# Output projection of a two-layer block split along its input, one half issued inside the recurrence

## The reference, cut to what matters

```python
fox_out = fox_attention(...)                       # features 0..511 of the mixer
rec, _  = hgrn2_chunkwise(gq, gf, gi, lb)          # the recurrence: 4 heads of 128, features 512..1023
rec = rmsnorm(rec, hgrn_norm_g) * silu(gg)
h = h + concatenate([fox_out, rec], -1) @ w_out    # 1024 x 1024, 512 tokens: the output projection
mem_n = rmsnorm(mem, norm_mem_g)                   # 256 memory tokens
h = h + memory_cross_attention(rmsnorm(h, norm_x_g), mem_n, w_xq, w_xkv, w_xo)
```

## Time and profile before

| | |
|---|---|
| median of 3 runs | 2276.75 us (2276.06 to 2281.61) |
| the profiled execution, its own time | 2282.82 us |
| its span in the profile | 2281.1 us |
| granted clock over the span | 0.963 |
| PE busy | 2130.7 us, 93% |
| DVE, ACT, POOL busy | 1157.3, 713.1 and 866.5 us |
| recurrence, first product to last head output | 267.7 to 344.9 us |
| norm of its heads | to 361.9 us |
| projection by `w_out` | to 410.2 us |
| units of `w_xkv` | to 465.5 us |

### The profile page before, as it was taken

The page is one execution under the profiler, slowest core; times in us unless marked ns, Lnnn a source line. Parts: engine busy times, 40 slices in busy tenths (PEclk is TensorE's granted clock), DMA queues, the critical chain, the costliest instruction groups (busy, mean ns, idle before and its releaser), DMA issues.

```text
span 2281.1 us, 26706 instructions
## 1 busy us (share of the span) xinstructions
PE 2130.7 (93%) x10150; PEld 1710.0 (75%) x10150; DVE 1157.3 (51%) x1880; ACT 713.1 (31%) x976; POOL 866.5 (38%) x456
## 2 busy tenths in 40 slices
PE   6999868999899999989988999999899988999998
PEld 5877667976678878865356888888788767888887
DVE  4145684524687886556536676632665664111112
ACT  4243533423322222333433212222344323213221
POOL 2322332641344444435022444444344433444442
PEclk8999888999999999988998999999999999999999
DMA  4322003430455553221014555522223112233222
GB/s 131 102 70 70 10 1 111 130 111 22 152 177 184 180 176 104 93 88 56 1 56 148 170 193 177 178 93 93 76 91 109 61 37 74 93 103 99 92 88 79
DMA packets 223966, 232.56 MB, mean 102 GB/s; under 512 B 4195, under 2 KB 218932, under 8 KB 223740
## 3 DMA queue, kind: packets, MB, share of 16 engines
q1 hardware_dynamic: 223868, 231.22, 31.1%
HBM read 228.96 MB, written 2.24 MB: 101 GB/s over the span
## 4 chain that ended last, share of the span: by engine, by line
PE 81%; DVE 10%; ACT 3%; issue 3%; POOL 1%; DMA 1%; SPq 0%; DVEq 0%; ACTq 0%; PEldq 0%
PE ps L1836 23%; PE ps L1838 22%; PE ps L1837 22%; POOL wL L582 1%; PE ps L2326 1%; PE ps L1946 1%; PE ps L1964 1%; ACT wH L707 1%; PE ps L2340 1%; DVE adacc L1494 1%; PE ps L2047 1%; PE ps L2067 1%; DVE hnL L1165 1%; PE ps L1913 1%; DVE T L1178 1%
## 5 line engine op out<-in xcount | busy, mean ns | idle before, releaser
L582 POOL TENSOR_TENSOR wL<-raw,wH 128x1024 fp32r<-128x1024 f32 (+2 forms) x322 | 772.9, 2422 | 1268.2 <-ACT wH L707 1268.1
L1836 PE MATMUL ps<-hnH,wH 128*128 128x512 f32 x1344 | 540.0, 402 | 22.2 <-DVE hnL L1165 14.1
L1838 PE MATMUL ps<-hnH,wL 128*128 128x512 f32 x1344 | 530.6, 395 | 0.0
L1837 PE MATMUL ps<-hnL,wH 128*128 128x512 f32 x1344 | 530.2, 395 | 0.0
L707 ACT ACTIVATE wH<-raw 128x2048 fp32r<-128x2048 f32 (+2 forms) x161 | 302.5, 1879 | 554.8 <-PE ps L1838 528.3
L1836 PE MATMUL ps<-uH,wH 128*128 128x512 f32 x864 | 341.7, 395 | 9.2 <-DVE uL L1163 8.8
L1838 PE MATMUL ps<-uH,wL 128*128 128x512 f32 x864 | 338.3, 392 | 0.0
L1837 PE MATMUL ps<-uL,wH 128*128 128x512 f32 x864 | 338.3, 392 | 0.0
L1836 PEld LDWEIGHTS ps<-hnH,wH 128*128 128x128 f32 x1344 | 257.3, 191 | 81.8 <-issue 19.4
L1838 PEld LDWEIGHTS ps<-hnH,wL 128*128 128x128 f32 x1344 | 256.5, 191 | 55.6
L1837 PEld LDWEIGHTS ps<-hnL,wH 128*128 128x128 f32 x1344 | 257.0, 191 | 52.7 <-issue 1.2
(11 more groups left out here) (345 smaller groups left out, 2414.1 us busy)
## 6 DMA issues: line engine op xcount, KB each, us to landing
raw<-in_ffn_w_dram SPq DMA_DIRECT2D x60, 1024.0 KB, 5.1
adaw<-in_ada_w_dram SPq DMA_DIRECT2D x48, 1024.0 KB, 7.2
raw<-in_w_dram SPq DMA_DIRECT2D x32, 1024.0 KB, 5.4
raw<-in_w_in_dram SPq DMA_DIRECT2D x14, 1024.0 KB, 5.4
raw<-in_od_w_in_dram SPq DMA_DIRECT2D x12, 1024.0 KB, 5.3
raw<-in_w_xkv_dram SPq DMA_DIRECT2D x8, 1024.0 KB, 5.4
raw<-in_ffn_w_dram SPq DMA_DIRECT2D x8, 768.0 KB, 4.2
raw<-in_ev_w_in_dram SPq DMA_DIRECT2D x5, 1024.0 KB, 5.2
```

Of the source, the lines that this page charges most:

```text
L582: nc.gpsimd.tensor_tensor(wL[n % 2][:, k0:k1, 0:c], raw[n % 2][:, k0:k1, 0:c], wH[n % 2][:, k0:k1, 0:c].bitcast(F32), ALU.subtract).then_i ...
L1836: nc.tensor.matmul(out_ap, wh, xh, start=first, stop=False)
L1837: nc.tensor.matmul(out_ap, wh, xl, start=False, stop=False)
L1838: return nc.tensor.matmul(out_ap, wl, xh, start=False, stop=last)
```

## The change

The four units of `w_out` become eight of half the input (4 chunks each), first the four over the forget-gate half, then the four over the recurrence's half. PE issues the first four inside the recurrence, from the generator `output_beside`: after each of the 32 products one chunk of one block, three matmuls of 128x512. Their blocks lie in banks 4 and 5, so the products of the levels go round banks 2 and 3 alone. DVE adds each of the 8 blocks to `xT` in the recurrence (`residual_beside`), and adds the 8 blocks of the second half behind it, 16 in all instead of 8. SP loads, and ACT and POOL split, one half unit per head there. The memory is loaded earlier, to another place, and squared by ACT in heads 1 and 2; its scaling by DVE moves ahead of the first residual. The second four units wait chunk by chunk (`chunks_of`) instead of for all. The memory's transposes stand behind units 0 and 1 of the second four.

```diff
@@ -62,8 +62,9 @@
     for c0 in (1024, 1280, 2056, 2312, 2568, 2824, 1544, 1800, 3080, 3336):
         add("w_in", 0, KC, c0, UC)
     stage("out")
-    for c0 in range(0, D, UC):
-        add("w_out", 0, KC, c0, UC)
+    for k0 in (0, KC // 2):
+        for c0 in range(0, D, UC):
+            add("w_out", k0, KC // 2, c0, UC)
...
+    if OUT_FILL[0] <= b < OUT_FILL[1]:
+        return 4 + b % 2
     return 4 + b % 2 if V_FILL[0] <= b < V_FILL[1] else b % 4
 
 
 def last_in_bank(b):
 
-    return b - 2 if FOX_FILL[0] <= b < FOX_FILL[1] or V_FILL[0] + 2 <= b < V_FILL[1] else b - 4
+    return b - 2 if FOX_FILL[0] <= b < OUT_FILL[1] or V_FILL[0] + 2 <= b < V_FILL[1] else b - 4
...
             sp.wait_ge(op_lo, Q0["mix"] + 4)
             sp.dma_start(lvl[:], a["levels"].rearrange("l s t -> s l t")).then_inc(lvl_in, 16)
-
-            sp.wait_ge(op_lo, Q0["mix"] + 8)
+            load(AT["out"][0] + 1)
             for mb in range(2):
                 sp.dma_start(mtok[:, mb, :], a["mem"][0, mb * P:(mb + 1) * P, :]).then_inc(mem_in, 16)
-            loads(AT["out"][0] + 1, AT["ff1"][0])
+            loads(AT["out"][0] + 2, AT["ff1"][0])
...
+                    if l == 2:
+                        low(AT["out"][0] + 1 + h)
...
-            lows(AT["out"][0] + 1, AT["ff1"][0])
+            lows(AT["out"][0] + 5, AT["ff1"][0])
...
+                    if l == 1:
+                        high(AT["out"][0] + 1 + h)
+                    if l == 5 and h in (1, 2):
+                        act.wait_ge(mem_in, 32)
+                        nc.scalar.activation(mdump[:], mtok[:, h - 1, :], ACT.Square, accum_out=mstat[:, h - 1:h]).then_inc(astep, 1)
+                        acts[0] += 1
...
+            act.wait_ge(astep, acts[0])
+            nc.scalar.activation(mstat[:, 4:6], mstat[:, 0:2], ACT.Sqrt, bias=eps, scale=1.0 / D).then_inc(m_root, 1)
...
-            n = AT["out"][0]
+            n = AT["out"][0] + 4
             high(n + 1)
-            act.wait_ge(mem_in, 32)
-            for mb in range(2):
-                chain(nc.scalar.activation(mdump[:], mtok[:, mb, :], ACT.Square, accum_out=mstat[:, mb:mb + 1]))
-            nc.scalar.activation(mstat[:, 4:6], mstat[:, 0:2], ACT.Sqrt, bias=eps, scale=1.0 / D).then_inc(m_root, 1)
+
+            def memory_high(js):
+                for j in js:
+                    high_op(Q0["mem"] + j, memH[:, j, :], mT[j % 2][:], (m_t, j + 1))
+
+            memory_high(range(0, 4))
             high(n + 2)
-            for half in range(2):
-                high(n + 3 + half)
-                for j in range(4 * half, 4 * half + 4):
-                    high_op(Q0["mem"] + j, memH[:, j, :], mT[j % 2][:], (m_t, j + 1))
-                squares("x", BLOCK0[n], range(2 * half, 2 * half + 2))
-            m = AT["xkv"][0]
+            memory_high(range(4, KC))
+            squares("x", BLOCK0[n], range(0, 2))
+            high(n + 3)
+            squares("x", BLOCK0[n], range(2, 4))
+            high(n + 4)
             squares("x", BLOCK0[n], range(4, 6))
-            high(m + 1)
+            high(n + 5)
...
-                                          ps[2 + e % 4][:].rearrange("p (c t) -> p c t", c=TB)).then_inc(h_at, 1)
+                                          ps[2 + e % 2][:].rearrange("p (c t) -> p c t", c=TB)).then_inc(h_at, 1)
...
+            def residual_beside(j):
+
+                bb = OUT_FILL[0] + j
+                dve.wait_ge(blk_done, bb + 1)
+                nc.vector.tensor_tensor(xT[:, j, :], ps[bank(bb)][:], xT[:, j, :], ALU.add).then_inc(blk_taken, 1)
...
+                    if l == 1 and h:
+                        residual_beside(2 * h - 1)
+                    if l == 5:
+                        residual_beside(2 * h)
...
+            residual_beside(KC - 1)
...
+            dve.wait_ge(m_root, 1)
+            chain(nc.vector.reciprocal(mstat[:, 2:4], mstat[:, 4:6]))
+            for mb in range(2):
+                nc.vector.tensor_scalar(mtok[:, mb, :], mtok[:, mb, :], mstat[:, 2 + mb:3 + mb], None, ALU.mult).then_inc(m_n, 1)
+            b = OUT_FILL[1]
             for j in range(KC):
                 residual(b + j, j)
-                if j == 1:
-                    dve.wait_ge(m_root, 1)
-                    chain(nc.vector.reciprocal(mstat[:, 2:4], mstat[:, 4:6]))
-                    for mb in range(2):
-                        nc.vector.tensor_scalar(mtok[:, mb, :], mtok[:, mb, :], mstat[:, 2 + mb:3 + mb], None, ALU.mult).then_inc(m_n, 1)
-                if j in (3, 5):
-                    for jj in range(2 * j - 6, 2 * j - 2):
+                if j in (1, 3):
+                    for jj in range(2 * j - 2, 2 * j + 2):
                         memory_chunk(jj)
-                if j in (3, 5):
-                    norm_add("x", j - 3)
-                    norm_add("x", j - 2)
-                if j == 6:
-                    norm_add("x", 4)
-                    norm_add("x", 5)
+                if j in (3, 5, 6):
+                    norm_add("x", {3: 0, 5: 2, 6: 4}[j])
+                    norm_add("x", {3: 1, 5: 3, 6: 5}[j])
...
+            def output_beside():
+
+                pe.wait_ge(mx_done, FOX_H * TB)
+                pe.wait_ge(op_lo, Q0["mix"] + 4)
+                for u in range(AT["out"][0], AT["out"][0] + 4):
+                    unit_ready(u)
+                    unit_whole(u)
+                    for c in range(2):
+                        b = BLOCK0[u] + c
+                        cs = slice(c * P, (c + 1) * P)
+                        bank_free(b)
+                        for k in range(KC // 2):
+                            ins = parts(ps[bank(b)][:], (wH[u % 2][:, k, cs], wL[u % 2][:, k, cs]), (uH[:, k, :], uL[:, k, :]),
+                                        k == 0, k == KC // 2 - 1)
+                            if k == KC // 2 - 1:
+                                ins.then_inc(blk_done, 1)
+                            yield
+
+            beside = output_beside()
...
-                    if e >= 4:
-                        pe.wait_ge(h_at, e - 3)
+                    if e >= 2:
+                        pe.wait_ge(h_at, e - 1)
...
+                    next(beside, None)
...
-            n = AT["out"][0]
-            feature_unit(n, uH, uL, need=all_chunks_of(Q0["mix"]))
-            for u in range(1, 4):
-                feature_unit(n + u, uH, uL)
-                if u == 3:
-                    break
-                pe.wait_ge(m_n, 2)
-                for j in range(4 * u - 4, 4 * u):
-                    if j >= 4:
-                        pe.wait_ge(op_lo, Q0["mem"] + j - 3)
-                    for mb in range(2):
-                        ins = nc.tensor.transpose(ps[4 + j % 4][:, mb * P:(mb + 1) * P], mtok[:, mb, j * P:(j + 1) * P], ident)
-                    ins.then_inc(m_tr, 1)
+                broadcast(hrs[:, 4 * h:4 * h + 4], (5, 6, 7, 4)[h]).then_inc(h_bc, 1)
+
+            n = AT["out"][0] + 4
+            for u in range(4):
+                feature_unit(n + u, uH[:, KC // 2:KC, :], uL[:, KC // 2:KC, :], need=chunks_of(Q0["mix"] + 4) if u == 0 else None)
+                if u < 2:
+                    pe.wait_ge(m_n, 2)
+                    for j in range(4 * u, 4 * u + 4):
+                        if j >= 4:
+                            pe.wait_ge(op_lo, Q0["mem"] + j - 3)
+                        for mb in range(2):
+                            ins = nc.tensor.transpose(ps[4 + j % 4][:, mb * P:(mb + 1) * P], mtok[:, mb, j * P:(j + 1) * P], ident)
+                        ins.then_inc(m_tr, 1)
```

More of the change, by code:

```diff
@@ L120 @@
 FOX_FILL = (BLOCK0[FOX_UNIT], BLOCK0[AT["out"][0]])
+OUT_FILL = (BLOCK0[AT["out"][0]], BLOCK0[AT["out"][0] + 4])
 V_FILL = (BLOCK0[AT["od_in"][0] + 10], BLOCK0[AT["od_in"][0] + 13])
@@ L301, in bass_block_pair @@
     lvl = place("lvl", [P, 8, P], F32, AR + 8192)[0]
-    ho = place("ho", [P, HG_H, S], F32, AR + 12288)[0]
+    ho = place("ho", [P, HG_H, S], F32, AR)[0]
     dd = R + [place(f"dd{i}", [P, S], F32, HN + 2048 * i)[0] for i in range(HG_RING - 2)]
@@ L314, in bass_block_pair @@
     memL = place("memL", [P, KC, M_MEM], F32R, AR + 8192)[0]
-    mtok = place("mtok", [P, 2, D], F32, AR + 49152)[0]
+    mtok = place("mtok", [P, 2, D], F32, AR + 16384)[0]
     xk = place("xk", [P, KC, M_MEM], F32, AR + 16384)[0]
@@ L318, in bass_block_pair @@
     xq = place("xq", [P, KC, S], F32, AR + 32768)[0]
-    mdump = place("mdump", [P, D], F32, HN)[0]
+    mdump = place("mdump", [P, D], F32, AR + 12288)[0]
     xdump = place("xdump", [P, D], F32, AR + 20480)[0]
@@ L1426, in _ @@
                     dve.wait_ge(op_lo, Q0["mix"] + 4 + h - 1)
-                nc.vector.tensor_tensor(T[h % 2][:], ps[(5, 6, 7, 2)[h]][:], gg[:, h, :], ALU.mult).then_inc(op_t, 1)
+                nc.vector.tensor_tensor(T[h % 2][:], ps[(5, 6, 7, 4)[h]][:], gg[:, h, :], ALU.mult).then_inc(op_t, 1)
                 low_op(Q0["mix"] + 4 + h, uL[:, 4 + h, :], T[h % 2][:], uH[:, 4 + h, :])
@@ L2103, in _ @@
```

(20 more changed lines are left out.)

## The result

| | before | after |
|---|---|---|
| median of the runs | 2277.47 us (4 runs, 2276.06 to 2281.61) | 2264.16 us (4 runs, 2261.61 to 2266.47) |
| ratio, 95% interval | | 0.9933 [0.9918, 0.9948] |
| the profiled execution, its own time | 2282.82 us | 2266.47 us |
| its span, granted clock | 2281.1 us, 0.963 | 2264.8 us, 0.969 |

The change gains 13.3 us between the medians, 0.58%; by the ratio it is 0.67%. A second comparison, of 5 runs with 9, gave 2265.94 against 2278.16, ratio 0.9940 [0.9926, 0.9954].

What follows compares the result with a forecast made beforehand. DVE was taken to bound the recurrence, PE the projection, a buffer ring `w_xkv`. Recurrence +10.0, behind -22.9, `w_xkv` +0.5 gave -12.4 us: 2270.4 profiled, median 2264, range 2254 to 2274.

Steps and rivals of the forecast that it cites:

- additions: DVE in the recurrence: eight new additions of 0.69 us, seven on DVE's path, +4.8 us.
- lows: POOL in the recurrence: four half-size lows stretch DVE instructions with both inputs in SBUF, 1.5 us a head, +6.0 us.
- border of heads: PE in the recurrence: with two banks the diagonal step stands behind one more chunk, 0.5 us each, +1.5 us.
- faster clock: Recurrence: more matmuls bring PE's clock nearer 1, giving back a third of DVE's 7.1 us of waiting, -2.3 us.
- behind: Projection behind the recurrence: PE ends at 387.3 instead of 410.2, a gain of 22.9 us.
- `w_xkv`: Ring of buffers in the `w_xkv` units: half units leave less time to load ahead, 0.5 us lost, from 0 to 2.
- The three short waits: PE behind the recurrence: waits 1 us for `mtok`, 0.9 before unit 3 and 2.9 before unit 4.
- the offset of 6.1 us: Whole kernel: profiled execution lies 6.1 us above the median, so 2270.4 profiled becomes a median of 2264.
- Lows and clock cost nothing: Recurrence: low falls into POOL's gap, clock stays at 1, growth 4 us or less; gain 19, 2258; chance 0.22.
- PE bounds the recurrence: Recurrence: PE at half clock half of the time, growth 18 us; gain 4 to 5, 2272; chance 0.14.
- The second half is ACT's and DVE's: Projection's second half: memory chunks, squares, sums and roundings share 22 us, PE ends at 392; gain 7, 2269; chance 0.09.
- ACT stands still: Recurrence: ACT's rounding waits for PE, delaying what queues behind; slower if growth exceeds 22.4 us; chance 0.05.

Runs made afterwards that it cites:

- thin additions: Changed kernel with the eight residual additions in the recurrence cut to 8 of 512 tokens: recurrence 80.7 us, span 2259.5 us.
- thin lows: Changed kernel with POOL's four lows in the recurrence cut to 8 of 256 columns of each chunk: recurrence 79.6 us, span 2264.2 us.
- both thin: Changed kernel with both the lows and the additions of the recurrence cut to 8 columns and 8 tokens: recurrence 74.7 us, span 2253.4 us.
- matmuls alone: Kernel before, products round two banks, plus three unread matmuls after each of the 32 products: 2271.36 us, ratio 0.9983.
- all half units behind: Changed kernel with all eight half units behind the recurrence, their roundings, lows and additions there too: 2280.77 us, ratio 1.0003.

## Why the prediction was right, and where its terms were off

The forecast was 2264 (2254 to 2274), and 2264.16 was measured, faster by more than 0.3%. By its terms, all in us:

| term | forecast | measured | by what |
|---|---|---|---|
| additions | +4.8 | +3.5 to +4.9 | thin additions |
| lows | +6.0 | +4.6 to +6.0 | thin lows |
| border of heads, less the faster clock | -0.8 | -2.4, not clear of the norm's spread | both thin, 85.5 against 87.9 |
| recurrence with norm | +10.0 | +8.0 (6.9 to 8.7) | three profiles against two |
| behind | -22.9 | -22.2 | 26.3 against 48.5 |
| `w_xkv` | +0.5 | -1.5 | 54.4 against 56.0 |
| sum | -12.4 | -15.7 | |

*The mechanism held.* DVE bounds the recurrence (busy 91% of it), PE's matmuls went in without a wait, and the projection lost its first half. ACT's rounding waited for PE where the prediction said. It had its start at 304.3, when PE would be done with the block; it began at 307.62. The step was right and its time 3.3 us early: the product from which I counted stood at 303.43 and not at 300.4, for the levels ahead of it already carried additions and longer instructions, and from it to the rounding it was 4.2 us where I had counted 3.9.

*Behind.* The three short waits were forecast as 1.0, 0.9 and 2.9 us and measured 0.93, 0.84 and 2.62. `mtok` took 2.45 us for the pair. `mtok` was done 2.6 us behind the last `uL` (367.31 to 369.88) where I had 3.2, and the clock was at half behind the longest wait, which I had not counted: 7 matmuls in 3.12 us (386.55 to 389.67) instead of 1.6, 1.5 us. So the stage took 26.3 us where 25.5 was forecast.

*The clock.* The third of DVE's waiting (2.3 us) that I let it give back was the term with the weakest ground. DVE's wait for products was 7.1 and 3.8 us in the two profiles of before and 6.7 to 7.2 in the three of after, so it was not given back there. What the clock may have given is seen only over recurrence and norm together, 2.4 us with the matmuls alone, and is no more than the norm's own spread. The 0.5 us per border that I charged for two banks does not show.

*Two readings of the rows.* In the earlier trace rows the subtraction of 309.08 (1.16 us) ran beside POOL's multiply of 308.96, for `kd` only began at 309.65; the multiply of 310.16 (1.48 us) is the one beside `kd`. And the `mT` of 395.33 in the earlier trace rows lies behind POOL's low, which ended at 393.82. The trace has one beside the low, at 391.50, with 0.47 us, so what I said of instructions that read PSUM stands, as it does for the addition of 310.02.

*`w_xkv`.* The ring has the same steps as in the earlier trace rows: in the chain of after, ACT 1.93 and POOL 5.23 us. The 0.5 us of lateness did not show; instead the stage was 0.7 to 2.4 us shorter than in the two profiles of before (55.1 and 56.8), just below the 55 to 57 that I had named as a sign. The spread of the two is 1.7 us.

*The step that failed.* It is the one from the profile to the median. I let the offset of 6.1 us between the profiled execution and the median stand for both kernels. Before, it was indeed 5.3 us (2282.82 against 2277.47) and 7.1 (2285.29 against 2278.16); after, only 2.3 (2266.47 against 2264.16) and 0.7 (2266.65 against 2265.94). Between profiles the change gained 17.5 us (mean spans 2282.3 and 2264.8) where I forecast 12.4. The stages above give 15.7 of it, a start of the recurrence 1.4 us earlier another 1.4, and all that follows `w_xkv` 0.4. The earlier start is no work of the change: thin lows, with the change, began as late as before (267.6), and the matmuls alone, without it, as early as after (266.1). So the sum was off by 5 us and the offset by nearly as much the other way, and the hit to 0.2 us is luck. The offset is most likely the spread of the executions: 29 of the kernel before took from 2269.87 to 2284.05 us, and its two profiled ones, 2282.82 and 2285.29, lie at and just past the slow end of that. The clock of the second was lower than in eight of the nine runs beside it (0.961 against 0.964 to 0.968); where in the program those ran faster has no trace.

*The rivals.* "Lows and clock cost nothing" is out: the lows cost 4.6 us or more. "PE bounds the recurrence" is out at a clock of 0.98. "The second half is ACT's and DVE's" is out with 26.3 us, though its mechanism is what makes the third wait. "ACT stands still" happened three times, for at most 4.5 us, but exponentials late by that much were mostly covered: with both lows and additions thin, ACT still waits 3.8 us three times and does all its roundings, and the recurrence takes 74.7 us, against 74.2 with the matmuls alone.

## What to carry to other kernels

Look for a stage where the matrix engine is the one waited for, and a stage before it where another engine is and the inputs of some of that work are ready; moving the work was worth its full matmul time here (22.2 us for 96 matmuls of 0.227), less what its helpers (additions, splits) take on the engine that bounds the stage. Price those helpers by the instructions that they stretch on that engine, not by their own engine's idle time. Put a forecast against sums over stages that trade time with each other, profile the same code more than once before a difference of 2 us is called a gain, and don't carry the offset of one profiled execution over to the other kernel.

## What the runs showed of the hardware

96 extra matmuls whose result nobody reads cost the DVE-bound recurrence nothing: with its norm it took 85.0 us against 87.4, at a granted clock of 0.97 instead of 0.82, and the whole kernel had a ratio of 0.9983 [0.9968, 0.9998] to before. The gain itself is no larger than the spread of the norm. The norm, with 51 to 57 matmuls, takes 10.7 to 10.9 us at a clock of 0.71 to 0.73, 12.0 to 12.3 at 0.63 or 0.64, 13.2 and 13.3 at 0.61 and 0.62, and 13.9 at 0.50. Where a stretch of half clock falls thus moved 3 us between two neighbouring stages of the kernel before, and 2.5 us in and out of the norm of the changed one.

A rest of PE of 2.62 us was followed by half clock in the changed kernel, and one of 2.63 us in the kernel with all half units behind. Rests of 0.84, 0.93, 0.95 and, in the latter, 2.08 us were not: behind that last one the matmuls are 0.23 us apart (365.70 to 365.93). With the longest rest gone the projection and the stage behind it ran at 1.00.

Four POOL subtractions of two instructions each, 11.9 us, lengthened DVE's instructions in the same stretch by 3.9 us in all. Subtractions with both inputs in SBUF went from 0.68 to 1.29 and 1.75 us; masked copies (727 ns) and additions from PSUM (673 ns) were not longer.
